# Turned query tiles between gemm tiles, the indexer's relu and weighted sum in PSUM, and twelve top-k rounds ahead of the fox attention

## Chip, core and metric

One core of a Trainium2 chip runs the whole program. The metric is the device time of one execution in microseconds (us). The program is two transformer blocks on 512 tokens of width 1024, in float32, and it is one instruction stream for each engine: PE (TensorE) multiplies, DVE (VectorE), ACT (ScalarE) and POOL (GpSimd) do elementwise work, and SP (SyncE) issues nearly all DMAs. PSUM, where PE writes, has eight banks of 128 x 512 float32.

## What is computed

The part that the change touches is the first block's projection, its sparse branch's indexer, and the start of its forgetting ("fox") branch:

```python
h = rmsnorm(x, g_pre[i]); proj = h @ w_in[i]
(qa, ka, va, gate_a, qi, ki, wi, qb, kb, vb, fb, gate_b) = jnp.split(proj, offs, axis=-1)
# dsa branch, for each block of 128 queries
dots = jnp.einsum('bqhd,bsd->bqhs', qi_blk, ki)            # qi, ki after rope, 8 heads
score = jnp.einsum('bqhs,bqh->bqs', jax.nn.relu(dots), wi_blk)
score = jnp.where(causal[None], score, -jnp.inf)
_, sel = lax.top_k(score, 128)                             # then attention over the chosen keys
# fox branch, causal, 8 heads
logits = einsum(q, k) * scale + c_q - c_k                  # c = cumsum(log_sigmoid(fb + b_forget))
out = softmax(logits) @ v
```

The rest (the gated merge, the second block with a window attention and a latent attention, and its feed-forward part) is the same in both kernels.

## The kernel before

Every matrix product keeps float32 accuracy by splitting both factors in a high part (fp32r, a copy by ACT) and a low part (what is left, by DVE or POOL), and by three matmuls: high x high, high x low, low x high. Weights come in chunks of up to 128 x 2048 through a ring of two buffers. For chunk c SP loads `w_raw` (L541), ACT writes `w_hi` (L700), POOL writes `w_lo` as `w_raw - w_hi` (L616), PE multiplies (L1542). A chunk is loaded when the low part of chunk c-2 is done, and `w_hi` of c waits for PE to be through with c-2. Chunk numbers here: 4 is `sm` (the indexer's keys and weights, the forget gate, `ka`, `va`), 5 and 6 are `qb`, 7 and 8 `kb`, 9 and 10 `vb`, 11 and 12 `ga`. The first chunk of a unit is multiplied step by step over four banks (a step is three matmuls into one bank), the last one bank after another, so that a bank is full every twelve matmuls. Banks 0 to 3 hold `qb`, `kb` and `vb` in turn, and banks 1 and 2 then `ga`.

The orders of all engines are written out by hand; each engine works its own list in order and waits on counters. Around the change the lists are these:

- PE: `sm`; all of `qb`; eight turned tiles `t.qi` (four 128 x 128 transposes each, L1567) and two `t.ki`; 24 units `idx` of the indexer (three query blocks for each of eight heads, two matmuls each of 256, 384 or 512 columns, L1670) in banks 4 to 7; two turned tiles `t.ka`; the cumulative sum `cum` (L1678); all of `kb`; all of `vb`; eight steps of `ga`; then fox. Fox has 32 units (eight heads of four query blocks); the next projections' steps stand between its units, one in each from unit 2 on.
- ACT: the evacuation of `sm`; exp and ln of the forget gate; `w_hi` of chunk 6; the high part of the rope'd queries (`spI`, L791); `w_hi` of chunk 7; the evacuation of `qb`; the high parts of ki, ka and va (L796); 24 relus from PSUM to a ring of five buffers `sp` (L836); `w_hi` of 8 and 9; `cum` and `kb`; `w_hi` of 10 and 11; the high part of `vb` (L844).
- DVE: rope of the queries; the forget gate; rope of ki and ka; the low part of the queries (L1166); the copies of the turned tiles (L1090); the low parts of ka and va; 24 weighted sums into the score table `sc` (`tensor_scalar` for the first head, L1250, then `scalar_tensor_tensor`, L1253); three additions of the causal mask (L1258); the copies of `t.ka`; ten rounds of top-k (L1268 and L1272; a round is a max8 and a match_replace over each of three blocks and takes out eight keys of every row, and 16 rounds are needed); `split_pair(0)` (two casts, L1150, the high parts of the first pair of fox heads); the low parts of `vb` (L1284), each of which frees a bank; then fox's softmax. Three rounds follow fox, three more the rope of `qa`.
- POOL: `w_lo` of chunks up to 8; `qb` times the row scale (L625); `w_lo` of 9 and 10; `kb` times the row scale; `w_lo` of 11; the low parts of the first pair of heads (L662); `w_lo` of 12; then the scaling of fox's probabilities.
- SP: after chunk 12 it stacks the heads by twelve DMAs (`stack_head`, L554 and L555) once the pair's low parts are there; heads 2 and 3 follow when pair 1 is split.

Pair 1 is split by DVE after the fox unit that `PAIR_HI_AT` maps to 1, and its low part by POOL after the unit in `PAIR_LO_AT`. DVE first waits there until both heads of pair 0 have landed, since the casts overwrite their source.

Of the kernel before, what the change touches and what calls it, by code (L numbers as in the profile page):

```python
# [25 lines left out]
P = 128  # L26
# [188 lines left out]
PAIR_HI_AT, PAIR_LO_AT = {1: 1, 5: 2, 13: 3}, {0: 1, 3: 2, 11: 3}  # L215
ROUNDS_FIRST, ROUNDS_NEXT = 10, 3
# [69 lines left out]
def build(nc, dram, out):  # L286
    ctx = ExitStack()
    with ctx:
# [3 lines left out]
        def sem(name):  # L292
            return ctx.enter_context(nc.semaphore(name))
# [139 lines left out]
        scored, idx_done, chosen = sem("scored"), sem("idx_done"), sem("chosen")  # L433
# [43 lines left out]
        def bank_of(stage, i):  # L477
            return bank[USE[stage][i][0]]
# [211 lines left out]
        def _(act):  # L690
# [122 lines left out]
            for b in range(NB):  # L813
                evac("sm", b, sm[:, b, :], src=bank_of("sm", b)[:, 0:SM_W], scale=rT[:, b:b + 1])

# [4 lines left out]
            hi_through(UNITS["sm"][0] + UNITS["sm"][1] + 1)  # L820
            split_high(tmI, spI, 1)
# [3 lines left out]
            act.wait_ge(roped, 3)  # L825
            twice_high(kdI[:, 0], sm[:, :, SM_KI:SM_KI + DH])
# [198 lines left out]
        def _(dve):  # L1025
# [191 lines left out]
            rope_blocks(tm4, H, 8, "1", rp)  # L1217
            for b in range(NB):
                wait_emptied(dve, "sm", b)
# [7 lines left out]
            split_low(tmI, spI)  # L1227
# [15 lines left out]
            for i in range(24):  # L1243
                h, b = i // 3, 1 + i % 3
                lo, hi = span[b]
                dve_in = sp[:, i % RING, 0:hi - lo]
                w = sm[:, b, SM_WI + h:SM_WI + h + 1]
                wait_emptied(dve, "idx", i)
                if h == 0:
                    dve.tensor_scalar(sc[:, lo:hi], dve_in, w, None, ALU.mult).then_inc(idx_done, 1)  # L1250
                else:
# [24 lines left out]
            top_rounds(ROUNDS_FIRST)  # L1276
# [21 lines left out]
            top_rounds(TOPK // 8 - ROUNDS_FIRST - ROUNDS_NEXT)  # L1298
# [189 lines left out]
        def _(pe):  # L1488
# [164 lines left out]
            gemm("qb", aH, aL, False)  # L1653
# [3 lines left out]
            for j in range(H):  # L1657
                turn_tile("t.qi", j, lambda b: spI[:, b, j, :].bitcast(F32))
            pe.wait_ge(split_lo, NB + 2)
            for j in range(2):  # L1660
                turn_tile("t.ki", j, lambda b: kdI[:, j, b, :].bitcast(F32))
# [19 lines left out]
            gemm("kb", aH, aL, False)  # L1681
# [153 lines left out]
```

## Times and profile before

| | |
|---|---|
| runs | 1278.8, 1284.99, 1284.03 us (median 1284.03) |
| profiled execution | 1282.76 us, span 1281.0 us |
| PE busy | 1223.6 us, 96% of the span |
| PE weight loads | 1019.7 us, 80% |
| DVE, ACT, POOL busy | 624.8, 539.6, 542.1 us |
| chain that ended last | PE 83%, DVE 7%, POOL 3% |
| HBM | 87 GB/s over the span |

The page's strips have 40 slices of 32 us. PE is at nine tenths or more in most of them; slices 3 and 5 (64 to 96 and 128 to 160 us) read 8, and the first reads 5. In the timeline a row begins with its start and its length in us; the bracket at its end is the idle time of the engine before it and what ended that. A row with x and a number merges neighbours of the same kind.

### The profile page before, as it was taken

What the parts mean: (1) busy time and instruction counts of PE and PEld (TensorE: products, weight loads), DVE (VectorE), ACT (ScalarE), POOL (GpSimd) and SP (SyncE); (2) the same over time, 40 slices, a digit from 0 to 9 for tenths busy, and PEclk for the clock granted to TensorE, in tenths of its full rate; (3) what the DMA queues carried; (4) which work ended last, traced back from release to release, by engine and by line L of the source; (5) the groups of instructions that cost most, each with busy time, mean ns of one, the idle gap of its engine ahead of it and who ended that gap; (6) DMA issues with size and microseconds to landing.
All of it is one profiled execution on the core that took longest, in us unless ns stands there. A gap on an engine that the chain in (4) does not pass through costs nothing.

```text
span 1281.0 us, 15910 instructions
## 1 busy us (share of the span) xinstructions
PE 1223.6 (96%) x5982; PEld 1019.7 (80%) x5982; DVE 624.8 (49%) x1447; ACT 539.6 (42%) x965; POOL 542.1 (42%) x288
## 2 busy tenths in 40 slices
PE   5989899999999989699899998999999999999997
PEld 4867688888888877589788887888878888888886
DVE  6569666665616446575872566592432313130003
ACT  5452465457532444445583455623332323222112
POOL 4216745245444333324353566244434343434441
PEclk9999999999999999799999999999999999999999
DMA  7212553302132422232201401432323333322221
GB/s 230 72 59 83 148 150 115 99 34 67 66 115 99 148 85 97 66 134 85 66 20 52 132 1 34 165 99 85 112 67 99 99 99 99 99 99 86 96 97 66
DMA packets 71083, 119.20 MB, mean 93 GB/s; under 512 B 5592, under 2 KB 33112, under 8 KB 70624
## 3 DMA queue, kind: packets, MB, share of 16 engines
q1 hardware_dynamic: 71008, 118.19, 28.5%
q8 instruction: 48, 0.79, 0.3%
q14 instruction: 27, 0.22, 0.0%
HBM read 107.67 MB, written 4.21 MB: 87 GB/s over the span
## 4 chain that ended last, share of the span: by engine, by line
PE 83%; DVE 7%; POOL 3%; issue 2%; ACT 2%; SPq 1%; DMA 1%; DVEq 0%; ACTq 0%; POOLq 0%
PE bank L1542 64%; PE bank L1802 9%; PE bank L1623 4%; PE bank L1591 2%; PE bank L1605 2%; DVE sc L1272 1%; POOL w_lo L633 1%; DVE m L1268 1%; PE bank L1567 1%; DVE tmp L1332 1%; POOL sc L647 1%; POOL w_lo L616 0%; ACT w_hi L733 0%; PE bank L1561 0%; PE bank L1554 0%
## 5 line engine op out<-in xcount | busy, mean ns | idle before, releaser
L616 POOL TENSOR_TENSOR w_lo<-w_raw,w_hi 128x2048 fp32r<-128x2048 f32 (+5 forms) x91 | 393.8, 4328 | 607.7 <-ACT w_hi L700 565.6
L1542 PE MATMUL bank<-aH,w_hi 128*128 128x512 f32 x800 | 319.0, 399 | 9.4 <-DVE aL L1344 3.9
L1542 PE MATMUL bank<-aH,w_lo 128*128 128x512 f32 x800 | 313.3, 392 | 0.0
L1542 PE MATMUL bank<-aL,w_hi 128*128 128x512 f32 x800 | 313.3, 392 | 0.0
L700 ACT ACTIVATE w_hi<-w_raw 128x2048 fp32r<-128x2048 f32 (+5 forms) x87 | 156.0, 1793 | 282.1 <-PE bank L1542 183.8
L1542 PEld LDWEIGHTS bank<-aH,w_hi 128*128 128x128 f32 x800 | 151.4, 189 | 40.1 <-issue 10.8
L1542 PEld LDWEIGHTS bank<-aH,w_lo 128*128 128x128 f32 x800 | 150.9, 189 | 32.4
L1542 PEld LDWEIGHTS bank<-aL,w_hi 128*128 128x128 f32 x800 | 151.1, 189 | 26.8
L1542 PE MATMUL bank<-w_hi,aH 128*128 128x512 f32 (+4 forms) x256 | 92.2, 360 | 20.1 <-POOL w_lo L616 9.5
L1542 PE MATMUL bank<-w_hi,aL 128*128 128x512 f32 (+4 forms) x256 | 90.1, 352 | 0.0
L1542 PE MATMUL bank<-w_lo,aH 128*128 128x512 f32 (+4 forms) x256 | 90.1, 352 | 0.0
L1035 DVE TENSOR_TENSOR fg<-bank,rB 128x512 f32<-128x512 f32 x22 | 15.1, 691 | 127.3 <-PE bank L1542 127.2
L1542 PE MATMUL bank<-uH,w_hi 128*128 128x512 f32 x192 | 74.8, 390 | 0.1
L1542 PE MATMUL bank<-uH,w_lo 128*128 128x512 f32 x192 | 74.7, 389 | 0.0
L1542 PE MATMUL bank<-uL,w_hi 128*128 128x512 f32 x192 | 74.7, 389 | 0.0
L1126 DVE TENSOR_TENSOR pT<-bank,pT 128x256 fp32r<-128x256 f32 (+3 forms) x128 | 58.7, 459 | 27.9 <-ACT pT L765 27.4
L1542 PEld LDWEIGHTS bank<-w_hi,aH 128*128 128x128 f32 x256 | 49.9, 195 | 28.1 <-issue 20.4
L765 ACT ACTIVATE pT<-bank 128x256 fp32r<-128x256 f32 (+3 forms) x128 | 52.7, 412 | 39.9 <-PE bank L1605 38.6
L1802 PE MATMUL bank<-w_hi,fH 128*128 128x512 f32 x176 | 68.6, 389 | 0.8 <-ACT xT L711 0.8
L1802 PE MATMUL bank<-w_hi,fL 128*128 128x512 f32 x176 | 68.5, 389 | 0.0
L1802 PE MATMUL bank<-w_lo,fH 128*128 128x512 f32 x176 | 68.5, 389 | 0.0
L1477 DVE TENSOR_TENSOR xT<-bank,xT 128x512 f32<-128x512 f32 x8 | 5.4, 690 | 110.8 <-PE bank L1802 110.8
(297 smaller groups left out, 2096.9 us busy)
## 6 DMA issues: line engine op xcount, KB each, us to landing
w_raw<-in_w_in SPq DMA_DIRECT2D x24, 1024.0 KB, 5.0
w_raw<-in_w_gate SPq DMA_DIRECT2D x22, 512.0 KB, 3.9
w_raw<-in_w_up SPq DMA_DIRECT2D x22, 512.0 KB, 4.8
w_raw<-in_w_down SPq DMA_DIRECT2D x11, 1024.0 KB, 4.8
w_raw<-in_w_merge SPq DMA_DIRECT2D x8, 1024.0 KB, 4.9
w_raw<-in_w_out SPq DMA_DIRECT2D x8, 1024.0 KB, 4.9
w_raw<-in_w_ple_gate SPq DMA_DIRECT2D x4, 1024.0 KB, 5.0
fK<-kbT SPq DMA_DIRECT2D x24, 128.0 KB, 2.7
```

Of the source, the lines that this page charges most:

```text
L616: pool.tensor_tensor(out=w_lo[:, c % 2, 0:n], in0=w_raw[:, c % 2, 0:n], in1=w_hi[:, c % 2, 0:n].bitcast(F32), op=ALU.subtract).then_inc(w_ ...
L633: ins = pool.tensor_tensor(out=w_lo[:, c % 2, at], in0=w_raw[:, c % 2, at], in1=w_hi[:, c % 2, at].bitcast(F32), op=ALU.subtract)
L647: pool.tensor_scalar(s, s, rsum[:, i:i + 1], 1.0, ALU.mult, ALU.mult).then_inc(scaled, 1)
L700: act.activation(w_hi[:, c % 2, 0:n], w_raw[:, c % 2, 0:n], ACT.Copy).then_inc(w_hi_ready, 1)
L765: act.activation(p_views(a, u, pt, 0), t_view(a, u), ACT.Copy).then_inc(p_hi, 1)
L1035: return dve.tensor_tensor(out=o, in0=a, in1=b, op=ALU.mult)
L1126: empties(dve.tensor_tensor(out=p_views(a, u, pt, 1), in0=t_view(a, u), in1=p_views(a, u, pt, 0).bitcast(F32), op=ALU.subtract), name + ". ...
L1542: ins = pe.matmul(o, l, r, start=(kk == 0 and m == 0), stop=(kk == total - 1 and m == 2), skip_group_check=True)
L1591: ins = pe.matmul(o, q, k, start=(m == 0), stop=(m == len(pairs) - 1))
L1605: ins = pe.transpose(o[:, at * P:(at + 1) * P], src, ident[:])
L1623: ins = pe.matmul(o[:, cols], values(h, kb, vp), probs, start=(kb == 0 and m == 0), stop=(kb == 2 and m == 2), skip_group_check=True)
L1802: ins = pe.matmul(bank_of("down", i)[:], l[:, kk, tok], r[:, k, col], start=(kk == 0 and m == 0), stop=(kk == NF - 1 and m == 2))
```

## The change

- `qb`'s last chunk (chunk 6) is multiplied one bank at a time with turned tiles in front: three `t.qi` before bank 0, three before bank 1, two `t.qi` and one `t.ki` before bank 2, the other `t.ki` before bank 3.
- The high and low parts of the queries are made earlier on ACT and DVE (between the evacuations of `sm`, and straight after the rope). The high part of ki moves in front of the evacuation of `qb`.
- The relu writes back into its PSUM bank, and DVE's `scalar_tensor_tensor` reads the bank and frees it. For the first head its addend is the causal mask, so the three mask additions go.
- One step of chunk 7 (`kb`) stands behind every third indexer unit, and the other eight steps follow the 24 units; `t.ka` and `cum` come between `kb`'s two chunks. ACT's `w_hi` of chunk 9 moves behind the evacuation of `cum`.
- Twelve rounds instead of ten stand ahead of fox: two, the copies of `t.ka`, eight, `split_pair(0)`, two, the low parts of `vb`. Two rounds follow fox and two the rope.
- Pair 1 is split after unit 3 (before: unit 1), its low part after unit 1 on POOL (before: unit 0).

```diff
-PAIR_HI_AT, PAIR_LO_AT = {1: 1, 5: 2, 13: 3}, {0: 1, 3: 2, 11: 3}
-ROUNDS_FIRST, ROUNDS_NEXT = 10, 3
+PAIR_HI_AT, PAIR_LO_AT = {3: 1, 5: 2, 13: 3}, {1: 1, 3: 2, 11: 3}
+ROUNDS_KA, ROUNDS_PAIR, ROUNDS_VB, ROUNDS_NEXT = 2, 8, 2, 2
...
-            for b in range(NB):
+            for b in range(2):
                 evac("sm", b, sm[:, b, :], src=bank_of("sm", b)[:, 0:SM_W], scale=rT[:, b:b + 1])
+            split_high(tmI, spI, 1)
+            for b in range(2, NB):
+                evac("sm", b, sm[:, b, :], src=bank_of("sm", b)[:, 0:SM_W], scale=rT[:, b:b + 1])
+            hi_through(UNITS["sm"][0] + UNITS["sm"][1] + 1)
...
             for i in range(24):
                 h, b = i // 3, 1 + i % 3
-                nk = (b + 1) * P
-                if i >= RING:
-                    act.wait_ge(idx_done, i - RING + 1)
+                dots = bank_of("idx", i)[:, 0:(b + 1) * P]
                 wait_filled(act, "idx", i)
-                empties(act.activation(sp[:, i % RING, 0:nk], bank_of("idx", i)[:, 0:nk], ACT.Relu), "idx", i)
+                act.activation(dots, dots, ACT.Relu).then_inc(relued, 1)
+            hi_through(UNITS["kb"][0] + 1)
+            evac("cum", 0, cT[:, :], src=bank_of("cum", 0)[0:H, :], scale=-8.0)
             ahead("kb")
-            evac("cum", 0, cT[:, :], src=bank_of("cum", 0)[0:H, :], scale=-8.0)
...
-                    dve.wait_ge(idx_done, i - 2)
-                    dve.scalar_tensor_tensor(out=sc[:, lo:hi], in0=dve_in, scalar=w, in1=sc[:, lo:hi],
-                                             op0=ALU.mult, op1=ALU.add).then_inc(idx_done, 1)
+                dve.wait_ge(relued, i + 1)
+                if h:
+                    wait_emptied(dve, "idx", i - 3)
+                empties(dve.scalar_tensor_tensor(out=sc[:, lo:hi], in0=bank_of("idx", i)[:, 0:hi - lo], scalar=w,
+                                                 in1=sc[:, lo:hi] if h else tab("causal")[:, (3 - b) * P:4 * P],
+                                                 op0=ALU.mult, op1=ALU.add), "idx", i)
...
-                ins = dve.tensor_tensor(out=sc[:, hi - P:hi], in0=sc[:, hi - P:hi], in1=tab("causal")[:, 3 * P:4 * P],
-                                        op=ALU.add)
-            for j in range(2):
-                evac("t.ka", j, kaS[:, j, :])
...
-            top_rounds(ROUNDS_FIRST)
+            top_rounds(ROUNDS_KA)
+            for j in range(2):
+                evac("t.ka", j, kaS[:, j, :])
+            top_rounds(ROUNDS_PAIR)
 
             dve.wait_ge(qb_scaled, 8)
             dve.wait_ge(cum_stored, 16)
             split_pair(0)
+            top_rounds(ROUNDS_VB)
...
+            for j in range(NB):
+                for t in range(3 * j, min(3 * j + 3, H)):
+                    turn_tile("t.qi", t, lambda b: spI[:, b, t, :].bitcast(F32))
+                if j >= 2:
+                    if j == 2:
+                        pe.wait_ge(split_lo, NB + 2)
+                    turn_tile("t.ki", j - 2, lambda b: kdI[:, j - 2, b, :].bitcast(F32))
+                part("qb", first + 1, j, aH, aL, False, None, 0, 0, CHUNKS[first + 1][0])
...
                 fills(ins, "idx", i)
+                if i % 3 == 2:
+                    kb(i // 3, i // 3 + 1)
+            kb(8, 16)
             pe.wait_ge(split_lo, NB + 4)
...
-            gemm("kb", aH, aL, False)
+            for j in range(NB):
+                part("kb", first + 1, j, aH, aL, False, None, 0, 0, CHUNKS[first + 1][0])
```

On PE, before, the end of `qb` (L1542), the turned tiles and the first scores stand in a row:

```order
L1542 MATMUL bank<-aH,w_lo 128x512
L1567 MATMUL bank<-ident,spI 128x128 x32
L1567 MATMUL bank<-ident,kdI 128x128 x8
L1670 MATMUL bank<-kiS,qiS 128x256 x2
L1670 MATMUL bank<-kiS,qiS 128x384 x2
L1670 MATMUL bank<-kiS,qiS 128x512 x2
L1670 MATMUL bank<-kiS,qiS 128x256 x2
```

On PE, after, at the end of `qb` (L1539 is the same line as L1542 before, L1681 as L1670):

```order
L1539 MATMUL bank<-aH,w_lo 128x512
L1681 MATMUL bank<-kiS,qiS 128x256 x2
L1681 MATMUL bank<-kiS,qiS 128x384 x2
L1681 MATMUL bank<-kiS,qiS 128x512 x2
L1539 MATMUL bank<-aH,w_hi 128x512
L1539 MATMUL bank<-aL,w_hi 128x512
L1539 MATMUL bank<-aH,w_lo 128x512
L1681 MATMUL bank<-kiS,qiS 128x256 x2
```

The 40 transposes have moved up in front of `qb`'s last four banks, and one step of `kb` stands behind each three score units.

On DVE, before, where the rounds end and fox is prepared (`tQ`, `tK` are the casts of `split_pair(0)`):

```order
L1272 MATCH_REPLACE sc<-m,sc 128x512
L1150 CAST tQ<-qbT 128x512
L1150 CAST tK<-kbT 128x512
L1284 SCALAR_TENSOR_TENSOR vbS<-bank,rT,vbS 128x512 x4
L1104 ISA sp,mx<-bank,cB 128x128
```

On DVE, after, at the same place (L1151, L1261, L1265 and L1281 are L1150, L1268, L1272 and L1284 before):

```order
L1151 CAST tQ<-qbT 128x512
L1151 CAST tK<-kbT 128x512
L1261 MAX m<-sc 128x8 x3
L1265 MATCH_REPLACE sc<-m,sc 128x256
L1265 MATCH_REPLACE sc<-m,sc 128x384
L1265 MATCH_REPLACE sc<-m,sc 128x512
L1261 MAX m<-sc 128x8 x3
L1265 MATCH_REPLACE sc<-m,sc 128x256
L1265 MATCH_REPLACE sc<-m,sc 128x384
L1265 MATCH_REPLACE sc<-m,sc 128x512
L1281 SCALAR_TENSOR_TENSOR vbS<-bank,rT,vbS 128x512 x4
```

Two rounds now stand between the casts and the low parts of `vb`.

## Rows read from the trace of the kernel before

**Rows 1.** The page: busy time by engine; clock granted to PE, by slice

```profile
PE 1223.6 (96%) x5982; PEld 1019.7 (80%) x5982; DVE 624.8 (49%) x1447; ACT 539.6 (42%) x965; POOL 542.1 (42%) x288
PEclk9999999999999999799999999999999999999999
```

**Rows 2.** Chain that ended last, 40 to 400 us: start, length, engine, line

```profile
75.70 4.88 DVE qiS L1090 x8
...
101.38 2.68 DVE sc L1258 x2
...
137.53 0.44 DVE tQ L1150
...
223.37 16.32 PE bank L1542 x72
```

**Rows 3.** Timeline of PE, 50 to 162 us

```profile
73.16 1.91 PE L1567 MATMUL bank<-ident,spI 128*128 128x128 f32 x16
...
82.02 11.39 PE L1670 MATMUL bank<-kiS,qiS 128*128 128x256 f32 x48 [1.93 <-DVE kiS L1090]
93.27 1.06 PE L1567 MATMUL bank<-ident,kdI 128*128 128x128 f32 x8
...
97.88 0.50 PE L1542 MATMUL bank<-aH,w_hi 128*128 128x512 f32 x1
...
147.01 0.42 PE L1591 MATMUL bank<-fK,fQ 128*128 128x128 f32 x2
...
160.66 0.44 PE L1591 MATMUL bank<-fK,fQ 128*128 128x128 f32 x2 [0.91 <-DMA fK<-kbT]
```

**Rows 4.** Stretches: length; busy PE, PEld, DVE, ACT, POOL; PE clock; DMA, GB/s

```profile
80.00:84.00 4.00, 2.07 (x7) 1.90 (x7) 3.58 (x10) 2.21 (x6) 0.00 (x0) 0.74 0.01 4
84.00:88.00 4.00, 4.00 (x21) 3.44 (x19) 3.33 (x7) 3.42 (x9) 0.00 (x0) 0.83 0.00 0
```

**Rows 5.** Timeline of DVE, 80 to 155 us

```profile
96.90 7.15 DVE L1258 TENSOR_TENSOR sc<-sc,cst 128x128 f32<-128x128 f32 x3
104.08 1.29 DVE L1090 CAST kaS<-bank 128x512 fp32r<-128x512 f32 x2
105.29 1.47 DVE L1268 MAX8 m<-sc 128x8 f32<-128x256 f32 x3
...
137.53 0.43 DVE L1150 CAST tQ<-qbT 128x512 fp32r<-128x512 f32 x1
...
142.50 0.75 DVE L1284 SCALAR_TENSOR_TENSOR vbS<-bank,rT,vbS 128x512 fp32r<-128x512 f32 x1 [1.97 <-ACT vbS L844]
...
150.87 0.43 DVE L1150 CAST qbT<-qbT 128x512 fp32r<-128x512 f32 x1 [2.31 <-DMA fK<-kbT]
```

**Rows 6.** Groups by form, 80 to 150 us: count, busy, mean ns

```profile
L1253 DVE SCALAR_TENSOR_TENSOR sc<-sp,sm,sc 128x512 f32<-128x512 f32 x7 | 5.2, 750 | 0.1
L1284 DVE SCALAR_TENSOR_TENSOR vbS<-bank,rT,vbS 128x512 fp32r<-128x512 f32 x4 | 2.9, 747 | 2.1 <-ACT vbS L844 2.1
L836 ACT ACTIVATE sp<-bank 128x512 f32<-128x512 f32 x8 | 4.9, 614 | 0.4 <-PE bank L1670 0.4
```

**Rows 7.** Timeline of POOL, 95 to 156 us

```profile
96.59 4.72 POOL L616 TENSOR_TENSOR w_lo<-w_raw,w_hi 128x2048 fp32r<-128x2048 f32 x1 [27.46 <-ACT w_hi L700]
...
132.95 4.62 POOL L616 TENSOR_TENSOR w_lo<-w_raw,w_hi 128x2048 fp32r<-128x2048 f32 x1 [0.43 <-ACT w_hi L700]
...
153.88 1.28 POOL L662 TENSOR_TENSOR kbT<-kbT 128x512 fp32r<-128x512 f32 x1
```

**Rows 8.** Timeline of ACT, 130 to 133 us

```profile
130.95 1.92 ACT L700 ACTIVATE w_hi<-w_raw 128x2048 fp32r<-128x2048 f32 x1 [8.15 <-PE bank L1542]
```

**Rows 9.** A copy inside SBUF beside POOL, 436 to 443 us: DVE

```profile
438.06 3.65 DVE L1044 COPY ssum<-sq 128x512 f32<-128x512 f32 x1 [13.00 <-ACT sq L718]
```

**Rows 10.** The same stretch: POOL

```profile
436.82 4.61 POOL L616 TENSOR_TENSOR w_lo<-w_raw,w_hi 128x2048 fp32r<-128x2048 f32 x1 [6.16 <-ACT w_hi L700]
```

More of the change, by code:

```diff
@@ L432, in build @@
         lf_in, lf_ln = sem("lf_in"), sem("lf_ln")
-        scored, idx_done, chosen = sem("scored"), sem("idx_done"), sem("chosen")
+        relued = sem("relued")
         qb_scaled = sem("qb_scaled")
@@ L819, in _ @@
             act.activation(lf[:, 1, :], lf[:, 1, :], ACT.Ln, bias=1.0).then_inc(lf_ln, 1)
-            hi_through(UNITS["sm"][0] + UNITS["sm"][1] + 1)
-            split_high(tmI, spI, 1)
+            act.wait_ge(roped, 3)
+            twice_high(kdI[:, 0], sm[:, :, SM_KI:SM_KI + DH])
             ahead("qb")
@@ L824, in _ @@
                 evac("qb", j, qbT[:, j, :])
-            act.wait_ge(roped, 3)
-            twice_high(kdI[:, 0], sm[:, :, SM_KI:SM_KI + DH])
             wait_filled(act, "t.ki", 1)
@@ L1217, in _ @@
             rope_blocks(tm4, H, 8, "1", rp)
+            split_low(tmI, spI)
             for b in range(NB):
@@ L1226, in _ @@
                 rope_blocks(sm[:, :, o:o + DH].rearrange("p b (h d) -> p b h d", h=1), 1, 8, "1", rp)
-            split_low(tmI, spI)
             twice_low(kdI[:, 1], kdI[:, 0], sm[:, :, SM_KI:SM_KI + DH])
@@ L1245, in _ @@
                 lo, hi = span[b]
-                dve_in = sp[:, i % RING, 0:hi - lo]
                 w = sm[:, b, SM_WI + h:SM_WI + h + 1]
-                wait_emptied(dve, "idx", i)
-                if h == 0:
-                    dve.tensor_scalar(sc[:, lo:hi], dve_in, w, None, ALU.mult).then_inc(idx_done, 1)
-                else:
-                    dve.wait_ge(idx_done, i - 2)
-                    dve.scalar_tensor_tensor(out=sc[:, lo:hi], in0=dve_in, scalar=w, in1=sc[:, lo:hi],
-                                             op0=ALU.mult, op1=ALU.add).then_inc(idx_done, 1)
-            dve.wait_ge(idx_done, 24)
-            for b in range(1, NB):
-                lo, hi = span[b]
-                ins = dve.tensor_tensor(out=sc[:, hi - P:hi], in0=sc[:, hi - P:hi], in1=tab("causal")[:, 3 * P:4 * P],
-                                        op=ALU.add)
-            link(ins)
-            for j in range(2):
-                evac("t.ka", j, kaS[:, j, :])
+                dve.wait_ge(relued, i + 1)
[4 more added lines that the diff above has]
+                                                 op0=ALU.mult, op1=ALU.add), "idx", i)
+            for i in range(21, 24):
+                wait_emptied(dve, "idx", i)
             def top_rounds(n):
@@ L1297, in _ @@
             split_low(tmA, spA)
-            top_rounds(TOPK // 8 - ROUNDS_FIRST - ROUNDS_NEXT)
+            top_rounds(TOPK // 8 - ROUNDS_KA - ROUNDS_PAIR - ROUNDS_VB - ROUNDS_NEXT)
             link(dve.tensor_scalar(sc[:], sc[:], TAKEN * 0.9, NEG, ALU.is_gt, ALU.mult))
@@ L1652, in _ @@
             gemm("sm", aH, aL, True)
-            gemm("qb", aH, aL, False)
+            first = UNITS["qb"][0]
+            for k in range(CHUNKS[first][0]):
+                for j in range(NB):
+                    part("qb", first, j, aH, aL, False, None, 0, k, k + 1)
             pe.wait_ge(cst_landed, 32)
@@ L1656, in _, with kb @@
             pe.wait_ge(split_lo, NB)
[L1657 to L1661, printed above, removed]
+            for j in range(NB):
[6 more added lines that the diff above has]
+                part("qb", first + 1, j, aH, aL, False, None, 0, 0, CHUNKS[first + 1][0])
+            first = UNITS["kb"][0]
+            kb_steps = [(k, j) for k in range(CHUNKS[first][0]) for j in range(NB)]
+            def kb(at, to):
+                for k, j in kb_steps[at:to]:
+                    part("kb", first, j, aH, aL, False, None, 0, k, k + 1)
             for j in range(H):
@@ L1680, in _ @@
             fills(ins, "cum", 0)
-            gemm("kb", aH, aL, False)
+            for j in range(NB):
+                part("kb", first + 1, j, aH, aL, False, None, 0, 0, CHUNKS[first + 1][0])
             gemm("vb", aH, aL, True)
```

## The prediction

> **What bounds the kernel now.** I read the page first: PE is busy 96% of the span, the next engine half of it [rows 1]. So time is won only where PE stands or runs slow. The chain that ended last, in order of time, says where: PE carries it up to 73 us, then come DVE's copies of the turned tiles, the indexer, DVE's mask additions and ten top-k rounds up to the cast at 137.53, and fox's preparation; from about 161 us on it is mostly PE's again [rows 2]. PE's timeline over that stretch gives the price: the scores start at 82.02 after a wait of 1.93, they take 11.39, `kb` begins at 97.88, fox at 147.01, and fox's third head (unit 8) at 160.66, after a wait for its DMA [rows 3]. Unit 8 is my milestone. Behind it PE waited for nothing longer than 0.4 us up to 320 us, and all that feeds it there is triggered by PE itself, so what is gained at unit 8 stays gained at the end.
>
> **The turned tiles.** Sixteen transposes that wait for nothing take 1.91 us, 0.12 each [rows 3]; the 40 of them cost 4.8 us wherever they stand. Before, `qb` ended where they begin, at 73.16, and the scores began at 82.02, 8.86 later: 4.1 us are waits for the copies. After, the copies lie beside `qb`'s last banks (2.7 us each), so the scores can begin at 73.16 + 4.8 = 77.96. The queries' low parts must be there at 62.2, where chunk 5 ends (96 matmuls at 0.227 us, from 16.32 / 72 [rows 2], were 21.8, and half are still to come). The rope ends at 48.5 and the low parts take 2.5, so they are hidden with 10 us to spare. **Gain 4.1 us.**
>
> **The indexer.** Before, scores to `t.ka` took 11.25 us (82.02 to 93.27 [rows 3]). Three units have 2304 columns, 0.96 us at 2.4 GHz, so 7.7 would do; the rest is the handing over and the clock, which was granted at 0.74 and 0.83 in 80 to 88 us, after PE had stood [rows 4]. After, three units and one step of `kb` (3 x 0.227) cost PE 0.96 + 0.68 = 1.64 us. DVE needs for three sums 1.59 (the distance of their pieces in the chain before), and ACT's relu at 614 ns for the widest [rows 6] is faster than either. I take DVE's sum from PSUM as no dearer than from SBUF, because the 512-wide one from a bank took 747 ns and the one from SBUF 750 [rows 6]. At the start ACT has still to make the high parts of ka and va (1.4 us) behind its last `qb` bank, so the fifth unit finds its bank busy: 1.8 us of waiting. E, the end of the 24 units with eight steps, is 77.96 + 1.8 + 8 x 1.64 = 92.9. Then eight steps (5.4) and the unchanged 4.6 for `t.ka` and `cum` (93.27 to 97.88 [rows 3]) with 0.2 for one more change of operands: `kb`'s second chunk starts at 103.1. Before, it was 97.88 + 48 x 0.227 = 108.8. **Gain so far 5.6 us.** Bounds: if the clock sinks again as in [rows 4], 0.26 x 4 + 0.17 x 4 = 1.7 less; if nothing waits at the start, 1.8 more.
>
> The Trainium skill speaks against this step: in "Perfetto Trace Analysis", Optimizing Scalar/DVE Operations, an access of DVE costs about 60 ns in SBUF and about 125 ns in PSUM. By it 24 sums would be 1.6 us dearer, an estimate from that page. The trace does not show it, with 747 ns against 750 [rows 6], so the sum goes without it.
>
> **DVE between the indexer and fox.** The last sum is done about 1.0 us after E (relu 0.6, sum 0.75, less the step of `kb` that hides part). The three mask additions (7.15 us [rows 5]) are gone. Rounds start at 93.9 instead of 105.29. Ten rounds took 105.29 to 137.53 = 32.24 [rows 5], and the copies of `t.ka` 1.21 (104.08 to 105.29). So DVE comes to `split_pair(0)` at 93.9 + 32.24 + 1.21 = 127.35, ten us earlier than before.
>
> **The step on which it turns.** Why did three 128-wide additions take 7.15 us? POOL's `w_lo` ran from 96.59 for 4.72 [rows 5, 7]. The same is seen elsewhere: a copy inside SBUF beside a `w_lo` took 3.65 us and ended 0.28 us behind it (436.82 + 4.61 = 441.43; 438.06 + 3.65 = 441.71) [rows 9, 10]. DVE's work from PSUM and its rounds are not held up (rounds keep their 3.22 us beside POOL). The casts of `split_pair(0)` are such copies. Before, they came at 137.53, just as `w_lo` of chunk 11 ended (132.95 + 4.62 = 137.57) [rows 5, 7]. After, that `w_lo` follows PE: chunk 9 is used up 5.6 us earlier, its `w_hi` goes from 130.95 to 125.3 [rows 8], and `w_lo` from 132.95 to 127.3. DVE arrives at 127.35. If it arrives less than 0.4 us ahead (both casts must be in) or up to 4.6 us behind, it stands until POOL is done at 131.9. I take that as the forecast, since the window is 5 us wide and the estimate lies in it, though at its edge.
>
> The Trainium skill has this as a rule ("SBUF — State Buffer", SBUF: two separate sides): the port pair that VectorE and GpSimd share is a lock, held for the whole instruction, against a DVE copy in a two-port mode or with two SBUF inputs. By it the cast ends behind the whole `w_lo`; the trace agrees, with 441.71 behind 441.43 [rows 9, 10].
>
> Then: casts done at 132.7, two rounds to 139.1, and only now the low parts of `vb`, 0.65 apart; `ga`'s first bank is bank 1, free with the second of them at 140.4. PE is through `vb` at 103.1 + 144 x 0.227 = 135.8. Before it was 141.4, and DVE followed each bank at once (it waited 1.97 for the last [rows 5]). So **a new wait of 4.6 us stands ahead of `ga`**. Its eight steps are 5.45, and fox starts at 145.9 instead of 147.01: gain 1.1. Pair 0 is no wait: POOL's low parts (2.6) end at 134.7, and the twelve DMAs before it landed 10.1 later, so at 144.8, before head 1 is asked for at 149.2.
>
> **Fox's first units.** Before, DVE stood 2.31 us in front of unit 2 for the landing of pair 0 [rows 5]. Now pair 1 is split after unit 3. Unit 3's sum on DVE ends 3.6 us behind fox's start (147.01 to 149.84 for the start of unit 3, less 0.49 of a wait for `w_lo`, plus matmuls 0.7 and 0.6 on DVE). POOL then has the cast to wait for (0.4) and 2.6 of work, and from its end to PE's unit 8 it is 160.66 - 155.16 = 5.5 (six DMA issues and the landing) [rows 3, 7]. So unit 8 starts 12.1 behind fox's start, at 158.0, where before it was 13.65: PE would be there at 9, and stands 3 us. **Gain at unit 8: 2.7 us.** Of the clock's 1.7 I expect a quarter, 0.4. Sum: 2.3.
>
> What is moved behind fox is hidden: one round less ahead of the rope, where DVE idled 6 us for `qa`, and one less behind it, where it idled 2.6 us for `gb`.
>
> **Which time that is.** The profiled execution took 1282.76 us (span 1281.0). Less 2.3 it is 1280.5. The runs' median is 1284.03, 1.3 above it, and the runs spread over 6 us; from the median it is 1281.7. I say **1281**. Its own range, with the clock's 1.7, the 1.8 of the first wait and 2 us of spread, is 1277.5 to 1284.5.
>
> **Rivals.**
> *The casts slip in before POOL.* If DVE comes 0.5 us earlier or chunk 9 is later by as much, nothing stands: rounds end at 133.8, the second low part of `vb` is done at 135.1, and `ga` does not wait. Fox starts at 135.8 + 5.45 = 141.3, unit 8 at 153.4, gain 7.2, less 0.4: about 1276. For it: my estimate is at the edge, 0.05 us from the start of `w_lo`. Against: 0.4 of the 5 us window is on that side, and every small delay of the sums (which start behind ACT's relu) moves DVE later while PE goes on. Chance 0.27.
> *The clock or the handing over eats the rest.* The scores' pace becomes 1.9 to 2.0 a triple or the clock sinks; `kb` is then 2 to 3 us later and with it all that follows: gain 0 to 1, 1283.5. For it: the bank now goes through three engines, where ACT alone freed it before. Chance 0.12.
> *Slower: the bank's round trip decides.* PE's units wait for a bank of four that relu and sum have both to leave, with a step of `kb` in order between. One unit through all is about 0.43 + 0.61 + 0.75 and three handings of 0.1 = 2.1 us; four banks make that 0.53 a unit, 1.6 a triple, just PE's pace. If handings cost so much that a triple takes 1.64 + d, all is later by 8d: it passes the kernel before at d = 0.3 and is 0.5% (6.4 us) slower at d = 1.1, a trip of 3.7 us. At d = 1.3 the time is 1283 - 2.3 + 10.4 = 1291. Nothing in the trace shows handings of that size. Chance 0.06.
> *It doesn't do what it says*: the turned tiles wait for the low parts after all. They would have to be 10 us late. Chance 0.02, at 1284.
> The forecast has what is left, 0.53.
>
> **How the numbers follow.** This measurement can't tell changes under 0.5% (6.4 us) from none; faster means below 1277.6. The free-port rival is there two times in three (0.18), the forecast one time in nine with the spread of the runs (0.06), so faster 0.25; slower 0.06; the same 0.69. The range for 8 in 10 takes the free-port case in and leaves the slow one out: 1274 to 1286.
>
> **What would show it.** In the changed kernel's trace: the scores start at about 78, `kb`'s second chunk at 103, the first round at 94 (each right within 1 us, or that step is wrong). The cast of `tQ` is the test: long (about 4.6 us, ending behind `w_lo` of chunk 11) with PE idle some 4 us ahead of `ga`, released by DVE's `vbS`, in the forecast; 0.43 long and no such idle time in the rival. Unit 8 waits for the DMA of `fK` by about 3 us in both. Sums from PSUM much over 0.75 us for 512 columns, or a clock under 0.9 in 80 to 90 us, would make the indexer's term wrong. The whole is wrong if PE's idle time returns behind 161 us, where I say that nothing changes.

## The result, and the profile after

| | before | after |
|---|---|---|
| median of 20 runs each | 1281.2 us | 1285.83 us |
| profiled execution, its span | 1282.76, 1281.0 | 1284.86, 1283.1 |
| mean clock granted to PE in that execution | 0.985 | 0.983 |

The ratio after / before is 1.0034 (95% interval 1.0024 to 1.0043): the change costs some 4.4 us. I had forecast 1281 from a median of 1284.03 in three runs, a gain of 2.3; the median of 20 runs of the kernel before is lower, so against that base the forecast stands for 1279 (1281.2 less 2.3). The sign was wrong.

The page shows little: PE has 1224.4 us of matmuls where it had 1223.6 [rows 1].

```profile
PE 1224.4 (95%) x5982; PEld 1021.4 (80%) x5982; DVE 623.9 (49%) x1444; ACT 540.3 (42%) x965; POOL 542.4 (42%) x288
PEclk9999899999999999799999999999999999999999
```

In the fifth slice (128 to 160 us) the clock reads 8 now, where it read 9. PE's timeline of the changed kernel goes with [rows 3]. The two traces start differently: the second spreading matmul (`rB`), after which both do the same until the turned tiles, stands at 39.80 us before and at 36.95 after. The difference is one of executions and not of the change: over all fourteen traces of this case it stands between 36.95 and 41.03 us (both ends from kernels that are the same up to `ga`), in two of the kernel before at 39.80 and 37.45. So 2.85 us has to be added to a position after, to compare it with one before.

```profile
36.95 1.02 PE L1558 MATMUL bank<-rB,ones 128*128 128x512 f32 x2
...
74.87 1.21 PE L1681 MATMUL bank<-kiS,qiS 128*128 128x256 f32 x6
...
78.29 1.25 PE L1681 MATMUL bank<-kiS,qiS 128*128 128x384 f32 x4 [1.28 <-DVE sc L1251]
...
96.97 3.60 PE L1692 MATMUL bank<-cst,lf 128*8 128x512 f32 x8
100.50 0.50 PE L1539 MATMUL bank<-aH,w_hi 128*128 128x512 f32 x1
...
133.04 0.39 PE L1539 MATMUL bank<-w_hi,aL 128*128 128x512 f32 x1
137.79 0.77 PE L1539 MATMUL bank<-aH,w_hi 128*128 128x512 f32 x1 [4.36 <-DVE vbS L1281]
138.36 0.63 PE L1539 MATMUL bank<-aL,w_hi 128*128 128x512 f32 x1
138.78 0.63 PE L1539 MATMUL bank<-aH,w_lo 128*128 128x512 f32 x1
...
145.63 0.39 PE L1539 MATMUL bank<-aH,w_lo 128*128 128x512 f32 x1
145.86 0.33 PE L1588 MATMUL bank<-fK,fQ 128*128 128x128 f32 x2
...
158.78 0.44 PE L1588 MATMUL bank<-fK,fQ 128*128 128x128 f32 x2 [2.48 <-DMA fK<-kbT]
...
160.31 0.78 PE L1539 MATMUL bank<-aH,w_hi 128*128 128x512 f32 x1
```

The rows at 133.04 and 137.79 are the new stand (a time in which PE waits) ahead of `ga`. What follows is the surprise: starts 0.43 apart (138.36 to 138.78), where `vb`'s matmuls had 0.23. The stretches say why, in the columns of [rows 4]:

```profile
133.00:137.00 4.00, 0.43 (x2) 0.01 (x1) 3.92 (x11) 3.51 (x3) 0.97 (x1) 0.92 0.77 179
137.00:141.00 4.00, 3.21 (x8) 2.56 (x9) 1.96 (x3) 0.26 (x1) 3.57 (x1) 0.50 0.67 151
141.00:145.00 4.00, 4.00 (x15) 3.18 (x14) 0.00 (x0) 0.00 (x0) 0.00 (x0) 0.73 0.84 228
156.00:160.00 4.00, 1.52 (x11) 1.11 (x10) 1.18 (x8) 1.30 (x3) 2.02 (x4) 1.00 0.80 215
160.00:164.00 4.00, 4.00 (x16) 3.05 (x15) 2.04 (x11) 1.53 (x6) 1.18 (x2) 0.57 0.66 163
```

PE worked 0.43 of 4 us, and then the granted clock was 0.50, the lower of its two levels (1.2 GHz). The recorded stretch at half clock lasts 6.8 us, from 136.3 to 143.2. The 24 matmuls of `ga` took 8.07 us (137.79 to 145.86) in place of 5.45. A second stretch at half clock, of 3.4 us, stands behind the wait at unit 8.

DVE and POOL did what the prediction's turning step said ([rows 5, 7] of before):

```profile
91.57 1.48 DVE L1261 MAX8 m<-sc 128x8 f32<-128x256 f32 x3
...
125.02 4.52 DVE L1151 CAST tQ<-qbT 128x512 fp32r<-128x512 f32 x1
129.46 0.42 DVE L1151 CAST tK<-kbT 128x512 fp32r<-128x512 f32 x1
129.80 1.47 DVE L1261 MAX8 m<-sc 128x8 f32<-128x256 f32 x3
...
136.24 2.73 DVE L1281 SCALAR_TENSOR_TENSOR vbS<-bank,rT,vbS 128x512 fp32r<-128x512 f32 x4
```

```profile
124.64 4.61 POOL L616 TENSOR_TENSOR w_lo<-w_raw,w_hi 128x2048 fp32r<-128x2048 f32 x1 [0.82 <-ACT w_hi L700]
```

The cast of `tQ` (0.43 us in [rows 5]) takes 4.52 and ends 0.29 us behind POOL's `w_lo` (124.64 + 4.61 = 129.25). Two rounds follow, and the low parts of `vb` begin 3.2 us after PE's last `vb` matmul started.

### The profile page after: what moved, and what is told of

Its sections match the earlier page's. It is cut to its first block, busy times and chain, and to the rows that moved or that the text cites. A ratio compares the mean times of both kernels' runs of the same rounds, so it can differ in the third digit from the quotient of the medians.

```text
span 1283.1 us, 15891 instructions
## 1 busy us (share of the span) xinstructions
PE 1224.4 (95%) x5982; PEld 1021.4 (80%) x5982; DVE 623.9 (49%) x1444; ACT 540.3 (42%) x965; POOL 542.4 (42%) x288
## 4 chain that ended last, share of the span: by engine, by line
PE 86%; DVE 5%; POOL 4%; issue 2%; ACT 2%; DMA 0%; SPq 0%; DVEq 0%; ACTq 0%; POOLq 0%
PE bank L1539 66%; PE bank L1817 9%; PE bank L1620 4%; PE bank L1588 2%; PE bank L1602 2%; PE bank L1564 1%; POOL w_lo L633 1%; POOL w_lo L616 1%; DVE tmp L1329 1%; POOL sc L647 1%; PE bank L1681 1%; ACT w_hi L733 0%; PE bank L1558 0%; PE bank L1551 0%; POOL kbT L625 0%
## 5 line engine op out<-in xcount | busy, mean ns | idle before, releaser
L1539 PE MATMUL bank<-aH,w_hi 128*128 128x512 f32 x800 | 321.7, 402 | 13.3 <-DVE vbS L1281 4.4
L1539 PE MATMUL bank<-aH,w_lo 128*128 128x512 f32 x800 | 315.2, 394 | 0.0
L1539 PE MATMUL bank<-aL,w_hi 128*128 128x512 f32 x800 | 315.1, 394 | 0.0
L1539 PEld LDWEIGHTS bank<-aH,w_hi 128*128 128x128 f32 x800 | 152.8, 191 | 44.6 <-issue 15.0
L1539 PEld LDWEIGHTS bank<-aH,w_lo 128*128 128x128 f32 x800 | 151.9, 190 | 33.0
L1539 PEld LDWEIGHTS bank<-aL,w_hi 128*128 128x128 f32 x800 | 152.5, 191 | 27.0
L1539 PE MATMUL bank<-w_hi,aH 128*128 128x512 f32 (+4 forms) x256 | 91.6, 358 | 18.9 <-POOL w_lo L616 9.5
L1539 PE MATMUL bank<-w_lo,aH 128*128 128x512 f32 (+4 forms) x256 | 89.5, 350 | 0.0
L1539 PE MATMUL bank<-w_hi,aL 128*128 128x512 f32 (+4 forms) x256 | 89.3, 349 | 0.0
L1036 DVE TENSOR_TENSOR fg<-bank,rB 128x512 f32<-128x512 f32 x22 | 15.1, 691 | 127.3 <-PE bank L1539 127.3
L1539 PE MATMUL bank<-uH,w_hi 128*128 128x512 f32 x192 | 74.8, 390 | 0.0
L1539 PE MATMUL bank<-uH,w_lo 128*128 128x512 f32 x192 | 74.7, 389 | 0.0
L1539 PE MATMUL bank<-uL,w_hi 128*128 128x512 f32 x192 | 74.7, 389 | 0.0
L1539 PEld LDWEIGHTS bank<-w_hi,aH 128*128 128x128 f32 x256 | 49.5, 193 | 26.8 <-issue 22.0
```

Source lines behind the costliest of these rows:

```text
L1036: return dve.tensor_tensor(out=o, in0=a, in1=b, op=ALU.mult)
L1539: ins = pe.matmul(o, l, r, start=(kk == 0 and m == 0), stop=(kk == total - 1 and m == 2), skip_group_check=True)
```

## Experiments

My theory (A): the change is worth about what was forecast as long as PE runs at full speed; the stand ahead of `ga`, made by the held cast and by the two rounds behind it, lets the clock fall, and so does the shorter one at unit 8. Rivals: the slow `ga` has another cause (B), the loss is in the indexer or in the sums from PSUM (C), the hold of the cast is not what makes the wait (D). All ratios are to the kernel before. Three segments of PE's timeline are compared, since they do not depend on how a trace starts: from the spreading matmul (`rB`) to the first score, from there to fox's first matmul ("scores to fox"), and from there to the first score of the attention behind fox ("fox to the next attention").

**1. Fill the stand ahead of `ga`.**

```diff
             gemm("vb", aH, aL, True)
+            pe.wait_ge(emptied[7], USE["fox.t"][1][1])
+            for k in range(19):
+                pe.matmul(bank[7][:], aH[:, k % KD, 0:P], aL[:, k % KD, :], start=True, stop=True)
             side("fox", 0, SIDE_FIRST["fox"])
```

> The changed kernel with 19 matmuls of 512 columns put into the stand ahead of ga: they write a bank that nothing reads (bank 7), take 19 x 0.227 = 4.3 us at full clock, and the stand was 4.36. Nothing else moves. Theory A (the stand is cheap, the clock behind it is not): PE no longer stands, the granted clock stays 1.00 from 136 to 143 us, ga starts where it did (137.8) and its eight steps take 5.45 us in place of 8.07, so fox starts at 143.2 in place of 145.86 and the whole is 2.6 us shorter than the changed kernel (about 1.4 to 2 us above the kernel before). Rival B (the matmuls' own wait for operands or banks made ga slow, not the clock): fox starts at 145.9 again, time unchanged.

Measured: 1284.27 us, ratio 1.0020 (1.0008 to 1.0032). PE's timeline and one stretch:

```profile
133.71 4.47 PE L1700 MATMUL bank<-aL,aH 128*128 128x512 f32 x19
138.23 0.47 PE L1539 MATMUL bank<-aH,w_hi 128*128 128x512 f32 x1
...
143.79 0.33 PE L1588 MATMUL bank<-fK,fQ 128*128 128x128 f32 x2
```

```profile
137.00:141.00 4.00, 3.95 (x18) 2.97 (x17) 2.40 (x4) 0.71 (x1) 4.00 (x1) 1.00 0.88 203
```

`ga` starts no earlier (0.44 later, as all positions of this trace are), and fox 2.07 earlier: `ga` takes 5.56 us. In the trace useless matmuls in the gap save 2.5 us; by the medians it is 1.6 (1285.83 to 1284.27), and the intervals of the two ratios overlap. B falls by the trace: the same matmuls on the same operands run at full speed.

**2. No round behind the casts.**

```diff
-ROUNDS_KA, ROUNDS_PAIR, ROUNDS_VB, ROUNDS_NEXT = 2, 8, 2, 2
+ROUNDS_KA, ROUNDS_PAIR, ROUNDS_VB, ROUNDS_NEXT = 2, 8, 0, 3
```

> The changed kernel with the two rounds between the casts and vb's low parts moved behind fox (ten rounds ahead of fox, three behind it, then three). Theory A: the cast is still held to 129.5 by w_lo, but the low parts of vb then follow PE's banks at once, ga starts at 133.4 in place of 137.8 and its matmuls run at 0.227; fox at 138.9 in place of 145.86 (7 us earlier). Unit 8 is bound by the landing of pair 0 (about 143.8), then cast, POOL and DMA: about 153 in place of 158.8. Time 5 to 7 us below the changed kernel, 1 to 2 below the kernel before. Rival C (the loss of the change lies in the indexer or the PSUM sums, not here): still slower than the kernel before by 3 us or more.

Measured: 1279.77 us, 0.9983 (0.9970 to 0.9996). From the first scores to fox 63.85 us, in place of 70.99. The hold is still there, and costs nothing ahead of `ga`:

```profile
128.03 4.52 DVE L1151 CAST tQ<-qbT 128x512 fp32r<-128x512 f32 x1
132.47 0.41 DVE L1151 CAST tK<-kbT 128x512 fp32r<-128x512 f32 x1
132.81 1.40 DVE L1281 SCALAR_TENSOR_TENSOR vbS<-bank,rT,vbS 128x512 fp32r<-128x512 f32 x2
```

C falls. Unit 8 came about where it was expected: its row stands at 155.41, but this trace starts 3.0 us later than that of the changed kernel (`rB` at 39.97), so that it is 152.4 in those terms, for 153. It still waited 2.48 us, and the half clock behind it stayed.

**3. The casts of pair 0 on ACT.**

```diff
             ahead("vb")                       # ACT
+            act.wait_ge(qb_scaled, 8)
+            act.wait_ge(cum_stored, 16)
+            for p, t in enumerate((qbT, kbT)):
+                act.activation(pair_hi(p, 0), t[:, 0, :], ACT.Copy).then_inc(pair_hi_ready, 1)
...
             dve.wait_ge(cum_stored, 16)       # DVE
-            split_pair(0)
```

> The changed kernel with the two casts of pair 0 done by ACT (2 x 0.6 us at 124.6) and not by DVE; the twelve rounds stay ahead of fox. Theory A (the port that DVE shares with POOL holds the cast for 4.5 us, and this hold is what makes the wait): DVE's rounds run through to 131.5, vb's low parts follow PE, ga starts at 133.4 with no stand and no fall of the clock; fox 138.9, unit 8 near 153; time 5 to 7 us below the changed kernel. Rival D (the two rounds more would make the stand anyway): a stand of 2 us or more stays ahead of ga.

Measured: 1279.92 us, 0.9981 (0.9970 to 0.9992), scores to fox 63.85. ACT's timeline; POOL's `w_lo` ran from 126.44 to 131.07 in it:

```profile
126.26 0.61 ACT L846 ACTIVATE tQ<-qbT 128x512 fp32r<-128x512 f32 x1
126.78 0.62 ACT L846 ACTIVATE tK<-kbT 128x512 fp32r<-128x512 f32 x1
```

The second copy lies wholly within POOL's `w_lo`, and the first ends in it. The same copies beside the same POOL instruction are not held when ACT makes them. With the hold gone, twelve rounds fit ahead of fox without a stand. D falls: it takes the hold and the rounds together. The Trainium skill ("SBUF — State Buffer", Who interferes with whom) says that PE and ACT never wait for that port; the trace agrees, with 0.61 against 4.52 us.

**4. Pairs split after the units of before.**

```diff
-PAIR_HI_AT, PAIR_LO_AT = {3: 1, 5: 2, 13: 3}, {1: 1, 3: 2, 11: 3}
+PAIR_HI_AT, PAIR_LO_AT = {1: 1, 5: 2, 13: 3}, {0: 1, 3: 2, 11: 3}
```

> The changed kernel with the units after which pairs are split as they were before (pair 1 high after unit 1, low after unit 0). Theory A: the stand ahead of ga stays (4.4 us and half clock); the cast of pair 1 comes at 147.3 in place of 149.5, and with it POOL's work and the six DMAs, so the wait of 2.5 us at unit 8 shrinks to 0 to 0.8 and the half clock behind it (3.4 us, worth about 1.3) is gone: 2 to 4 us below the changed kernel. Rival E (unit 8's wait is the queue of DMA issues and not the cast): the wait stays at 2 us or more, the time the same within 1 us.

Measured: 1283.54 us, 1.0010 (0.9994 to 1.0027). The wait at unit 8 went to 1.34 us (I had said 0 to 0.8), no half clock followed it, and from fox to the next attention it took 110.15 us in place of 113.39. The stand ahead of `ga` was the same (4.35 us), yet the half clock at it lasted 3.4 us here and not 6.8, and scores to fox took 70.04 in place of 70.99: nothing was changed there, so that is a difference of executions. By the times (1285.8 to 1283.5) and ratios (1.0034 to 1.0010) the new table of units costs 2 to 3 us of what the change loses; the intervals overlap, but experiment 6 gives the same amount once more. E falls by the wait, which shrank.

**5. Both repairs, and POOL's order.** As 3 and 4 together, with the twelve rounds ahead of fox kept, and POOL takes the low parts of pair 0 ahead of `w_lo` of chunk 11:

```diff
-            lo_through(UNITS["ga"][0])
             pool.wait_ge(qb_scaled, 8)
             split_pair(0)
             lo_through(UNITS["ga"][0] + 1)
```

> The changed kernel with three things other: ACT makes the two casts of pair 0, POOL takes their low parts ahead of w_lo of chunk 11 (and not behind it), and the units after which pairs are split are as before the change. Theory A: no stand ahead of ga (fox starts about 63.5 us behind the scores, as with the casts on ACT alone, against 71.0 in the changed kernel); pair 0 has landed 3.5 us earlier, so pair 1 is cast after unit 1 without waiting and unit 8 finds its operands: from fox's start to the next attention's scores about 109 us in place of 113.4 to 114.1. Sum 9 to 11 us below the changed kernel, 5 to 6.5 below the kernel before. Rival F (something else bounds fox's first units, the issues of the DMA queue in order): unit 8 still waits over 2 us and the time is that of the casts on ACT alone, 2.5 below the kernel before.

Measured: 1274.12 us in six runs, 0.9937 (0.9917 to 0.9956), the best version here, with less time than both kernels. Scores to fox 63.87, fox to the next attention 110.56 (I had said 109: unit 8 still waits 1.35, where the rival F had said over 2; F falls, by the time too).

**6. The change without its rounds and tables.** `ROUNDS_... = 2, 8, 0, 3` and the table of experiment 4.

> The changed kernel with ten rounds ahead of fox (none behind the casts) and the pairs split after the units of before: of the change the turned tiles and the indexer stay. Theory A: no stand ahead of ga, fox 63.8 us behind the scores; pair 0 is still late (DVE's cast held by POOL), so unit 8 waits 1 to 2.5 us; 1277 to 1278.5, some 4 to 5 below the kernel before. Rival C (the first two parts are worth nothing): as the kernel before within 1 us.

Measured: 1277.02 us, 0.9959 (0.9944 to 0.9974). So turned tiles and indexer are worth some 5 us together, and the third part of the change, the rounds and the table, loses 9 (1285.8 less 1277.0). Experiment 2 differs from this one in the table alone: 0.9983 against 0.9959 is 3 us for the table.

**7. The turned tiles alone**, in the kernel before (the edits at `qb`, at `split_low(tmI, spI)` and in ACT's list around `sm`):

```diff
-            gemm("qb", aH, aL, False)
+            first = UNITS["qb"][0]
+            for k in range(CHUNKS[first][0]):
+                for j in range(NB):
+                    part("qb", first, j, aH, aL, False, None, 0, k, k + 1)
...
+            for j in range(NB):
+                for t in range(3 * j, min(3 * j + 3, H)):
+                    turn_tile("t.qi", t, lambda b: spI[:, b, t, :].bitcast(F32))
```

> The kernel before with the turned tiles between qb's last tiles, and nothing else of the change. My step: scores start 4.1 us earlier; DVE's chain and PE's both move by that, the casts come at 133.4 just as w_lo ends, so all of it is kept: 4 us below the kernel before, and up to 1.7 more where the clock no longer falls at the start of the scores (PE stood 1.4 and 1.9 us there before). Rival G (the gain is lost again ahead of fox, because DVE and not PE sets the pace there): within 1 us of the kernel before.

Measured: 1279.35 us, 0.9978 (0.9964 to 0.9991). By the ratio that is 2.8 us, less than the 4 I had expected. From the spreading matmul to the scores it takes 37.92 us in place of 42.22, a gain of 4.3, and from there to fox 65.19. The first trace of the kernel before has 64.99 for that, but with a half clock at the scores; its second trace (experiment 12) has none there and 63.68. So at full clock 1.5 of the 4.3 us are lost again, and PE's timeline shows them within the scores: from the first score to `t.ka` it takes 11.49 us here and 9.98 there, with a wait of 0.89 for ACT near the start that the other does not have. What is left, 2.8, is what the time says. G falls.

**8. The indexer alone**, in the kernel before (relu and sum in PSUM, mask in the first sums, `kb` steps between the scores):

```diff
-                empties(act.activation(sp[:, i % RING, 0:nk], bank_of("idx", i)[:, 0:nk], ACT.Relu), "idx", i)
+                act.activation(dots, dots, ACT.Relu).then_inc(relued, 1)
...
+                if i % 3 == 2:
+                    kb(i // 3, i // 3 + 1)
+            kb(8, 16)
```

> The kernel before with relu and sum in PSUM, the mask within the first sums, and half a chunk of kb between the scores; turned tiles, rounds and tables as before. My step: PE gains 1.5 us up to kb's second chunk, DVE gets to the casts about 6 us earlier (131.4), just ahead of w_lo of chunk 11 (131.4) or held by it to 136; either way the low parts of vb are in time. 1 to 2 us below the kernel before. Rival H (the sums from PSUM and the round trip of the banks cost more than they bring): scores to t.ka longer than 21 us with the kb steps in it, and 1 us or more above the kernel before.

Measured: 1282.32 us, 1.0000 (0.9982 to 1.0018). Expected were 1 to 2 us. In the trace scores to fox take 62.71 us: 2.3 less than in the first trace of the kernel before, but only 1.0 less than in its second (63.68), where the clock did not fall at the scores, as it did not here. H falls by the trace (scores to `t.ka` 19.5 us, not 21). The ratio, with an interval of 4.6 us, neither shows nor excludes 1.0, so the total stays open.

**9. Both stands filled.** Experiment 1, and ten matmuls into bank 0 ahead of unit 8.

```diff
+                        if i == 8 and name == "fox":
+                            wait_emptied(pe, "vb", 0)
+                            for k in range(10):
+                                pe.matmul(bank[0][:], aH[:, k % KD, 0:P], aL[:, k % KD, :], start=True, stop=True)
```

> The changed kernel with both stands of PE filled: 19 matmuls ahead of ga (as in the fill before) and 10 more (2.27 us) into a free bank ahead of fox's unit 8, where PE stood 2.48 for the DMA. Theory A (the clock falls after PE has stood, and costs half of what PE works at the lower speed): the half clock of 3.4 us behind unit 8 goes too; from fox's start to the next attention's scores 112.1 in place of 113.4, and the mean clock is back at that of the kernel before (0.986); the time 1.3 us below the first fill's, 3 to 4 below the changed kernel's: within 1.5 us of the kernel before. Rival I (the half clock behind unit 8 is set by the transfers or by chance, not by the stand): it stays, and the time is the first fill's (1284.3).

Measured: 1281.65 us, 0.9998 (0.9985 to 1.0011), and the mean clock over twelve runs 0.986, as in the kernel before. PE's timeline, and the stretch behind unit 8:

```profile
157.62 2.55 PE L1584 MATMUL bank<-aL,aH 128*128 128x512 f32 x10
160.34 0.44 PE L1592 MATMUL bank<-fK,fQ 128*128 128x128 f32 x2 [0.17 <-DMA fK<-kbT]
```

```profile
160.00:164.00 4.00, 3.83 (x22) 2.93 (x22) 2.32 (x11) 1.53 (x6) 1.28 (x2) 1.00 0.85 232
```

Unit 8 comes no earlier for it, and the kernel takes 2.6 us less than with one stand filled. By the time (the interval is 3.3 us wide) the whole loss of the change is gone, with every wait for data still in place. That speaks against I. The trace alone would not do it: the unfilled kernel's second trace (experiment 11) has no half clock behind unit 8 either.

**10. One round behind the casts.** `ROUNDS_... = 2, 8, 1, 3`.

> The changed kernel with one round between the casts and vb's low parts in place of two (eleven ahead of fox, three behind it). Theory A: the stand ahead of ga is 4.36 - 3.23 = 1.1 us; scores to fox 64.9 to 65.2 us if the clock holds at so short a stand, 66.5 to 67.8 if it falls. The second wait of one size with the first kernel's (1.3 us at the scores, no fall) makes me expect that it holds, with a chance of 0.7. Time 1280 to 1281.5, so most of the loss of two rounds (about 7 us) comes with the second of them.

Measured: 1281.02 us, 0.9991 (0.9979 to 1.0004). A stand of 1.12 us ahead of `ga`, the clock at 1.00 behind it, scores to fox 65.22. The first round costs 65.22 - 63.85 = 1.4 us, the second 70.99 - 65.22 = 5.8, of which 3.2 are the round and the rest is the clock.

**11 and 12. Both kernels once more**, for a second trace.

> The changed kernel as it is, for a second trace. Theory A: the half clock of 6.8 us where ga starts comes again (scores to fox 71 us), and the one behind unit 8. What is left open by the first trace, two more stretches in 700 to 800 us than a stand there explains, is chance if they stand elsewhere now, and the change's own if they stand in the same places.

> The kernel before as it is, for a second trace. If the first trace is typical, the half clock comes again at the start of the scores (scores to fox about 65 us) and nowhere from there to 480 us; where its stretches stand in 700 to 800 us tells how far these are chance; the first 40 us may differ by 3 us from run to run, as they did over the traces so far (the second spreading matmul at 37.0 to 40.2).

The changed kernel again has 6.8 us at half clock at `ga` (scores to fox 71.29), but none behind unit 8, though PE stood 2.46 us there. Of the six traces here with a wait of 2.46 to 2.50 us at unit 8 (those of after, of experiments 1, 2, 3 and 10, and this one) it is the only one without. The kernel before has none at the scores this time, though the waits are the same (1.38 and 1.93 us). The stretch from 81 to 85 us of both traces of before, the first trace first (the scores start at 82.02 and at 79.67 in them):

```profile
81.00:85.00 4.00, 2.98 (x10) 2.82 (x11) 3.04 (x10) 2.02 (x6) 0.00 (x0) 0.61 0.01 4
```

```profile
81.00:85.00 4.00, 4.00 (x24) 3.28 (x22) 3.85 (x9) 4.00 (x12) 0.00 (x0) 1.00 0.01 4
```

Between 700 and 800 us the second trace of before has two stretches at half clock (at 717.7 and 768.9) and that of after has one (at 769.7), the reverse of the first pair: there it is chance.

The segments of the main traces, in us:

| | spreading to scores | scores to fox | fox to next attention |
|---|---|---|---|
| before; again | 42.22; 42.23 | 64.99; 63.68 | 112.63; 112.31 |
| after; again | 37.92; 37.92 | 70.99; 71.29 | 113.39; 111.84 |
| one stand filled; both | 37.92; 37.92 | 68.48; 68.47 | 113.40; 111.85 |
| casts on ACT; and tables, POOL's order | 37.92; 37.92 | 63.85; 63.87 | 114.14; 110.56 |

## Why the prediction was wrong

Point by point, positions after given with the 2.85 us added:

| step | forecast | measured |
|---|---|---|
| first scores | 77.96 | 77.72 |
| wait for a bank at the scores' start | 1.8 | 1.28 |
| second chunk of `kb` | 103.1 | 103.35 |
| first round | 93.9 | 94.42 |
| DVE at the cast of `tQ` | 127.35 | 127.87 |
| `w_lo` of chunk 11 starts | 127.3 | 127.49 |
| low parts of `vb` start | 139.1 | 139.09 |
| stand ahead of `ga` | 4.6 | 4.36 |
| `ga` starts | 140.4 | 140.64 |
| `ga`'s eight steps | 5.45 | 8.07 |
| fox starts | 145.9 | 148.71 |
| unit 8 | 158.0 | 161.63 |

Up to the start of `ga` every step is right within 0.6 us, the new wait included. That the cast was held at all was near the edge, as the prediction said: DVE came 0.38 us behind the start of `w_lo`, and 0.8 us earlier both casts would have been in before it. The side on which it fell was in part luck. **The step that failed is the next one, "Its eight steps are 5.45"**: I priced the stand at its own length and gave the clock nothing. The prediction had seen such a price in [rows 4], where PE had stood and the clock was 0.74 and 0.83, but charged it at the scores only ("Of the clock's 1.7 I expect a quarter, 0.4", which brings its 2.7 down to 2.3). The rival on the clock looked there too, not behind the stand that the forecast itself had put ahead of `ga`. Measured, this term is 2.5 us (experiment 1: 70.99 against 68.48).

The other misses. Unit 8 was put 12.1 us behind fox's start; it came 12.9 behind (0.8 us), with a wait of 2.48 where 3 was said. The half clock behind it was not in the sum: 113.39 against 111.85 with the stand filled, 1.5 us. "What is gained at unit 8 stays gained": no idle time came back behind it, which was right, but at 720 to 724 us PE lost 1.7 us to the clock in the profiled execution (granted 0.57 of 4 us), after a wait of 1.8 that the kernel before has as well.

And the base: the first profile of before had its own half clock in it, 1.3 us (64.99 against 63.68 in its second trace), and 0.3 more behind fox's start (112.63 against 112.31). So the change's gain at full clock, measured from the spreading matmul to the next attention, is 218.22 (before again) less 218.24 (both stands filled), nothing. Of the forecast's 2.7 at unit 8, 1.6 were in that base, 0.8 are unit 8's, and 0.3 is fox's start (106.39 us behind the spreading matmul with both stands filled, 106.1 in the forecast). Without its rounds and its table the change does gain there: experiment 6 takes 213.60 us, 4.6 less than before again, with no half clock in it. The waits that the third part made ate that, and the clock did the rest.

On top of nothing come the falls of the clock. Behind the stand ahead of `ga` it fell in three traces of three, for 2.5, 2.8 and (experiment 4) 1.6 us over the filled one, 2.3 on average. Behind unit 8 it fell in five of six for 1.5 us, 1.25 on average. The kernel before had its fall of 1.3 us at the scores in one of three traces with those waits (experiment 8 keeps them), 0.4 on average. Together that is some 3 us of the 4.4, an estimate from few traces. All runs list their mean clock: 0.9826 over the 20 runs of after, 0.9863 over 35 of before, and 0.9856 over the 29 of before that go with experiments 5 to 8. The difference, 0.0030 to 0.0037 of 1283 us, is 3.9 to 4.7 us of work at full speed. That is an upper estimate of the loss, since a low clock costs nothing while PE waits, and it is about the whole difference; experiment 9 says the same. Where the rest beyond the two stands falls, the traces don't settle.

The weighed rule on PSUM came out as the rows had it: the 512-wide sum from a bank took 749 ns (groups by form, 60 to 150 us; [rows 6] has 750 from SBUF), so the Trainium skill's dearer access ("Perfetto Trace Analysis", Optimizing Scalar/DVE Operations) does not show in the time of such an instruction here.

```profile
L1251 DVE SCALAR_TENSOR_TENSOR sc<-bank,sm,sc 128x512 f32<-128x512 f32 x7 | 5.2, 749 | 0.0
L836 ACT ACTIVATE bank<-bank 128x512 f32<-128x512 f32 x8 | 4.6, 580 | 0.2 <-PE bank L1681 0.2
```

Of the rivals, none came: the casts did not slip in before POOL (DVE was 0.38 us late), and the banks' round trip made a triple of 1.74 us, not the 2.9 of the slow rival. The forecast's mechanism came, and the slowness with it.

## What to carry to other kernels

A wait on the busiest engine has two prices: its length, and the slow work behind it. Where a forecast puts a stand of several us on TensorE, take the price of the clock from the profile's own rows (here 1.6 to 2.8 us behind a stand of 4.4, 1.5 behind 2.5 in five traces of six, none behind 1.1 to 1.35) and add it, at every stand, in both kernels. One trace of the base is not enough for that: the same waits cost it 1.3 us in one execution and nothing in the next. Before filling another engine's idle time with work moved ahead, ask which wait it will be behind: here the first round more cost 1.4 us and the second 5.8. A copy that is held up by the port which VectorE and GpSimd share can go to ScalarE.

## What the runs showed of the hardware

- Whether the granted clock fell to 0.50 after one and the same wait differed between executions: after 1.38 and 1.93 us ahead of the scores in one trace of three, after 2.5 us at unit 8 in five of six. After 4.35 us ahead of `ga` it fell in three of three, for 6.8, 6.8 and 3.4 us. The Trainium skill ("TensorE: Matmul & The Clock Gate", What's actually happening) says that the number of slow matmuls at the start of a kernel varies from run to run; these traces show such a variation behind waits in the middle of one.
- Matmuls that write a bank nobody reads kept the clock at 1.00 and made the kernel faster than standing did: 1285.8, 1284.3 and 1281.65 us with none, one and two stands filled.
- ACT's copies of 512 columns took 0.61 us beside a `w_lo` of POOL that held DVE's for 4.52.
- The first 40 us differed by up to 4 us between executions, in one kernel by 2.35.
